# Bias rows stored head by head, four products in another order, sums ahead of splits, and a count of its own for one weight quarter, in a hybrid decoder layer on one Trainium2 core

## The reference

```python
h = rmsnorm(x, norm_g) * (1 + scale[:, None, :]) + shift[:, None, :]     # shift, scale, gate = split(c @ ada_w + ada_b)
q, kc, vc, ksl, vsl, kw, vw, gts, hc, bc, cc, z = split_proj(h @ w_in)
k_cmp, v_cmp = compress(kc, ...), compress(vc, ...)                      # silu(blocks @ w1) @ w2
o_attn = gates * (compressed attention, top-k selected attention, window attention)   # all with a T5 bias rel_bias
u = cc * hc
y_conv = bc * short_conv(u, conv_w)
x = x + gate * (concat([o_attn * silu(z_a), y_conv * silu(z_c)]) @ w_out)
y = rmsnorm(x, final_g)
```

## Time and profile before

| what | value |
|---|---|
| median of three runs | 1536.29 us (1535.63 to 1536.37) |
| the profiled execution | 1532.23 us |
| its span | 1530.4 us |
| TensorE matmul busy | 1433.0 us (94%) |
| VectorE, ScalarE, GpSimd busy | 964.0, 704.4, 234.7 us |
| chain that ended last | PE 80%, DVE 7%, DMA 5%, ACT 3% of the span |
| mean granted TensorE clock | 0.979 |

### The profile page before, as it was taken

One profiled execution on the slowest core, in us unless ns is written; L12 is line 12 of the kernel. 1 busy time (PEld: TensorE's weight loads), 2 busy tenths in 40 slices (PEclk: granted clock), 3 DMA queues, 4 the chain that ended last, 5 costly groups with the idle time before them and its releaser, 6 DMA issues.

```text
span 1530.4 us, 27904 instructions
## 1 busy us (share of the span) xinstructions
PE 1433.0 (94%) x10526; PEld 1236.4 (81%) x10526; DVE 964.0 (63%) x2312; ACT 704.4 (46%) x1546; POOL 234.7 (15%) x441
## 2 busy tenths in 40 slices
PE   5987998999999999969989999999999999999998
PEld 2876998999999999957767777777777766788886
DVE  2643768787787887848666666667567654653226
ACT  2421232423323223226567777777777765631111
POOL 1100010101101011031021242232222131000000
PEclk9998999999999999989999999999999999999999
DMA  9376123423333334297321141121121129963231
GB/s 345 99 137 126 28 84 90 117 60 96 86 75 105 78 90 112 62 316 237 111 91 43 29 108 56 43 70 47 33 57 30 30 74 357 265 207 98 82 98 35
DMA packets 169669, 164.76 MB, mean 108 GB/s; under 512 B 53644, under 2 KB 150028, under 8 KB 164160
## 3 DMA queue, kind: packets, MB, share of 16 engines
q1 hardware_dynamic: 153904, 94.11, 22.6%
q0 software_dynamic: 15632, 68.87, 14.9%
HBM read 131.27 MB, written 35.83 MB: 109 GB/s over the span
## 4 chain that ended last, share of the span: by engine, by line
PE 80%; DVE 7%; DMA 5%; ACT 3%; issue 3%; SPq 1%; DVEq 0%; POOL 0%; ACTq 0%
PE PS L1258 26%; PE PS L1619 11%; PE PS L1425 8%; PE PS L1390 7%; PE PS L1369 5%; PE PS L1307 4%; PE PS L1370 3%; PE PS L1472 2%; PE PS L1214 1%; DMA gw<-in_ada_w 1%; PE PS L1215 1%; PE PS L1216 1%; DMA adaw<-in_ada_w 1%; PE PS L1576 1%; DMA wr<-in_w_in 1%
## 5 line engine op out<-in xcount | busy, mean ns | idle before, releaser
L1258 PE MATMUL PS<-bo,wsl 128*128 128x264 f32 x4104 | 504.5, 286 | 11.1 <-DVE qp L2186 5.8
L1258 PEld LDWEIGHTS PS<-bo,wsl 128*128 128x128 f32 x4104 | 503.6, 190 | 12.2 <-DVE qp L2186 6.0
L1882 ACT ACTIVATE pr<-PS,nm 128x640 f32<-128x640 f32 (+7 forms) x256 | 181.0, 708 | 45.2 <-DVE nm L2392 42.6
L1715 ACT ACTIVATE wsl<-wsum 128x512 fp32r<-128x512 f32 x105 | 65.6, 630 | 231.9 <-DVE wsum L2107 231.9
L1905 ACT ACTIVATE ptt<-PS 128x512 f32<-128x512 f32 x264 | 149.6, 601 | 41.6 <-PE PS L1390 41.4
L1390 PE MATMUL PS<-ident,pr 128*128 128x128 f32 x1056 | 147.2, 274 | 0.0
L1425 PE MATMUL PS<-ptt,kvt 128*64 128x256 f32 x1056 | 136.7, 390 | 0.0
L1390 PEld LDWEIGHTS PS<-ident,pr 128*128 128x128 f32 x1056 | 122.4, 141 | 8.9 <-ACT ptt L1905 0.4
L1425 PEld LDWEIGHTS PS<-ptt,kvt 128*64 128x64 f32 x1056 | 66.9, 136 | 41.2 <-issue 16.5
L2392 DVE CUSTOM_DVE_ANT_0 PS<-PS,near,nm 128x256 f32<-128x256 f32 x192 | 94.7, 493 | 6.8
L2391 DVE TENSOR_REDUCE nm<-PS 128x1 f32<-128x128 f32 (+5 forms) x128 | 70.5, 551 | 39.2 <-PE PS L1370 38.7
(11 more groups left out here) (358 smaller groups left out, 2403.2 us busy)
## 6 DMA issues: line engine op xcount, KB each, us to landing
wr<-in_w_in SPq DMA_DIRECT2D x32, 512.0 KB, 5.6
adaw<-in_ada_w SPq DMA_DIRECT2D x8, 1024.0 KB, 9.5
wr<-in_w_in SPq DMA_DIRECT2D x32, 256.0 KB, 4.3
q_stacked<-qp POOLq DMA_DIRECT2D x64, 128.0 KB, 2.7
qb<-q_stacked SPq DMA_DIRECT2D x32, 256.0 KB, 3.1
mr<-mixed SPq DMA_DIRECT2D x16, 512.0 KB, 3.9
mixed<-yy POOLq DMA_DIRECT2D x16, 264.0 KB
xb<-in_x_prompt POOLq DMA_DIRECT2D x8, 512.0 KB, 4.7
```

Source lines behind the costliest of these rows:

```text
L1258: ins = pe.matmul(PS[:, 2 * q + c, 0:H // 2], w[:, x, kk, :], b[:, y, kk, c * H // 2:(c + 1) * H // 2], start=(first and kk == 0 and x == ...
L1882: act.activation(pr[r][:, h, 0:k], score_cols(b0, w), ACT.Exp, scale=-1.0, bias=nm[:, r, h:h + 1], accum_out=rsum[:, r, h:h + 1]).then_inc ...
```

## The change

The diff does five things. The line numbers of the changed file are some 9 to 14 higher than before's.

1. `rows` moves to partitions 64 to 79 of `kvs`, and the one store of 3072 KB becomes 16 stores of 192 KB, one for each head, issued by POOL in the pairs 4 to 19 (`store_bias(n - 4)` at step 4). ScalarE's wait for `row_st` is gone.
2. In pair 0 the first four products run in the order 2, 3, 0, 1. The wait for `kv_ev` moves to the second of them and that for `ada_ev` to the fourth.
3. The pieces of the sums: `ADDED` says at which step a piece is summed, `SPLIT` at which it is split. At a step the sum now comes ahead of the split of the piece before. Pieces 12 to 19 (now with O21 as 12 to 15 and O12 as 16 to 19) are summed before any of them is split, into `qp`, `ts`, `eg` and `er`; all have two instructions. The last split moves from step (3,2) to (2,6).
4. The first quarter of w1 of the keys counts on `wr_ld` (`load_w1(0, 0, wr_ld)`). TensorE waits for it ahead of step 0 and for the three others ahead of step 8.
5. The base of that semaphore in `wo_ld` falls from 64 to 48.

```diff
-        rows = sb("rows", [NH, XW], cx=cC)
...
+        rows = kvs[64:64 + NH, 0:XW]
...
-        wo_ld = list(zip(xp_ld + q_ld, [192, 192, 64, 64] + [128] * 4))
+        wo_ld = list(zip(xp_ld + q_ld, [192, 192, 48, 64] + [128] * 4))
...
-        PIECE = [(s_, k) for s_ in range(3) for k in range(HK)] + [(3, 2), (3, 3), (4, 2), (4, 3), (3, 0), (3, 1), (4, 0), (4, 1)]
-        PIECES = {(0, 0): 0, (0, 1): 1, (0, 2): 2, (0, 3): 3, (0, 4): 4, (0, 5): 5, (0, 6): 6, (0, 7): 7, (1, 0): 8, (1, 4): 9,
-                  (1, 5): 10, (1, 6): 11, (2, 2): 12, (2, 3): 13, (2, 4): 14, (2, 5): 15, (2, 6): 16, (2, 7): 17, (3, 0): 18, (3, 1): 19}
-        def op_scratch(x):
-            return (er, eg) if x % 2 else ts
+        PIECE = [(s_, k) for s_ in range(5) for k in range(HK)]
+        ADDED = {(0, 0): (0,), (0, 1): (1,), (0, 2): (2,), (0, 3): (3,), (0, 4): (4,), (0, 5): (5,), (0, 6): (6,), (0, 7): (7,),
+                 (1, 0): (8,), (1, 1): (9,), (1, 4): (10,), (1, 5): (11,), (1, 7): (16, 17), (2, 0): (18, 19), (2, 1): (12, 13), (2, 2): (14, 15)}
+        SPLIT = {(0, 1): (0,), (0, 2): (1,), (0, 3): (2,), (0, 4): (3,), (0, 5): (4,), (0, 6): (5,), (0, 7): (6,), (1, 0): (7,),
+                 (1, 1): (8,), (1, 4): (9,), (1, 5): (10,), (1, 6): (11,), (2, 3): (12, 13), (2, 4): (14, 15), (2, 5): (16, 17), (2, 6): (18, 19)}
+        def sum_ready(x):
+            return x + 1 if x < 12 else x + 5 if x < 16 else x - 3
+        def op_sum32(x):
+            if x < 12:
+                return (er if x % 2 else ts[0])[:, :]
+            return f32(qp[:, x - 12, :]) if x < 16 else (ts[1], eg, ts[0], er)[x - 16][:, :]
...
-            def load_w1(c, q):
+            def load_w1(c, q, landed=None):
                 src = (cmp_w1_k, cmp_w1_v)[c].rearrange("l (t p) c -> p (l t) c", p=P)
-                sp.dma_start(w1[c][:, 8 * q:8 * q + 8, :], src[:, 8 * q:8 * q + 8, :]).then_inc(xp_ld[2 + c], 16)
+                sp.dma_start(w1[c][:, 8 * q:8 * q + 8, :], src[:, 8 * q:8 * q + 8, :]).then_inc(landed or xp_ld[2 + c], 16)
...
-            load_w1(0, 0)
+            load_w1(0, 0, wr_ld)
...
-            po.wait_ge(tb_ev, 1)
-            rv = rows[:, :]
-            po.dma_start(rowd, bass.AP(rv.tensor, rv.offset, [list(rv.ap[0]), [0, P], [1, XW]])).then_inc(row_st, 16)
+            def store_bias(h):
+                rv = rows[h:h + 1, :]
+                po.dma_start(rowd[h:h + 1], bass.AP(rv.tensor, rv.offset, [list(rv.ap[0]), [0, P], [1, XW]])).then_inc(row_st, 16)
...
+                    if i == 4 and 4 <= n < 4 + NH:
+                        store_bias(n - 4)
...
-            pe.wait_ge(kv_ev, 2 * NTT)
...
-            pe.wait_ge(ada_ev, 8)
...
-                        k, op, out = PLAIN[i]
+                        k, op, out = PLAIN[(2, 3, 0, 1)[i] if n == 0 and i < 4 else i]
+                        if n == 0 and i == 1:
+                            pe.wait_ge(kv_ev, 2 * NTT)
+                        if n == 0 and i == 3:
+                            pe.wait_ge(ada_ev, 8)
...
-            pe.wait_ge(xp_ld[2], 64)
+            pe.wait_ge(wr_ld, raw_landed(NBLK - 1) + 16)
             for m in range(32):
+                if m == 8:
+                    pe.wait_ge(xp_ld[2], 48)
...
-                act.wait_ge(op_sum, x + 1)
-                if x >= 16:
-                    act.wait_ge(*made(2, 3))
-                elif x >= 12:
-                    act.wait_ge(*made(2, 3 if PIECE[x][0] == 4 else 1))
-                act.activation(bo[SUMS[PIECE[x][0]][0]][:, 0, PIECE[x][1], :], op_scratch(x)[0][:, :], ACT.Copy).then_inc(op_hi, 1)
+                s_, k = PIECE[x]
+                act.wait_ge(op_sum, sum_ready(x))
+                if x >= 12:
+                    act.wait_ge(*made(2, 3 if x >= 16 else 1))
+                act.activation(bo[SUMS[s_][0]][:, 0, k, :], op_sum32(x), ACT.Copy).then_inc(op_hi, 1)
...
-                    act.wait_ge(op_sum, 16 if half else 18)
+                    act.wait_ge(op_lo, 16)
...
-                    act.wait_ge(row_st, 16)
...
-                    if (n, i) in PIECES:
-                        op_high(PIECES[n, i])
+                    for x in ((ADDED if n < 2 else SPLIT).get((n, i if n < 2 else i + 1), ())):
+                        if (x < 12) == (n < 2):
+                            op_high(x)
...
-                t = op_scratch(x)
-                if x >= 2:
+                t, kept = op_sum32(x), f32(qp[:, k, :])
+                if 2 <= x < 12:
                     dve.wait_ge(op_lo, x - 1)
-                if x < 18:
-                    dve.wait_ge(op_kept, 1 if x < 12 else 2)
-                    first_, second = (f32(bo[a][:, 0, k, :]), f32(qp[:, k, :])) if s_ < 4 else (f32(qp[:, k, :]), f32(bo[b][:, 0, k, :]))
-                    link(dve.tensor_tensor(t[0][:, :], first_, second, op))
-                    dve.tensor_tensor(t[0][:, :], t[0][:, :], f32(bo[a if s_ < 4 else b][:, 1, k, :]), ALU.add).then_inc(op_sum, 1)
-                else:
-                    dve.tensor_tensor(t[0][:, :], f32(bo[a][:, 0, k, :]), f32(bo[b][:, 0, k, :]), op)
-                    link(dve.tensor_tensor(t[1][:, :], f32(bo[a][:, 1, k, :]), f32(bo[b][:, 1, k, :]), op))
-                    dve.tensor_tensor(t[0][:, :], t[0][:, :], t[1][:, :], ALU.add).then_inc(op_sum, 1)
+                if x >= 16:
+                    dve.wait_ge(op_lo, 12)
+                dve.wait_ge(op_kept, 1 if x < 12 else 2)
+                if 12 <= x < 16:
+                    dve.wait_ge(op_sum, 16)
+                own, first_, second = (b, kept, f32(bo[b][:, 0, k, :])) if s_ == 4 else (a, f32(bo[a][:, 0, k, :]), kept)
+                link(dve.tensor_tensor(t, first_, second, op))
+                dve.tensor_tensor(t, t, f32(bo[own][:, 1, k, :]), ALU.add).then_inc(op_sum, 1)
 
             def op_low(x):
-                (s_, k), t = PIECE[x], op_scratch(x)
+                s_, k = PIECE[x]
                 dst = bo[SUMS[s_][0]]
-                dve.wait_ge(op_sum, x + 1)
+                dve.wait_ge(op_sum, sum_ready(x))
                 dve.wait_ge(op_hi, 1 + x + 1)
-                dve.tensor_tensor(dst[:, 1, k, :], t[0][:, :], f32(dst[:, 0, k, :]), ALU.subtract).then_inc(op_lo, 1)
+                dve.tensor_tensor(dst[:, 1, k, :], op_sum32(x), f32(dst[:, 0, k, :]), ALU.subtract).then_inc(op_lo, 1)
...
-                    if (n, i) in PIECES:
-                        x = PIECES[n, i]
-                        if x:
-                            op_low(x - 1)
-                        if x == 12:
-                            whole(O11)
+                    for x in ADDED.get((n, i), ()):
                         op_add(x)
-                    if n == NPLAIN and i == 2:
-                        op_low(19)
+                    for x in SPLIT.get((n, i), ()):
+                        op_low(x)
+                    if n == 1 and i == 6:
+                        whole(O11)
```

More of the change, by code:

```diff
@@ L751, in _ @@
             sp.wait_ge(x3_t, 80)
-            sp.wait_ge(row_st, 16)
+            sp.wait_ge(row_st, 16 * NH)
             sp.dma_start(near[:, :, :], flat(rowd, P - 1, [(XW - 1, P), (P * XW, NH), (1, 2 * P)])).then_inc(c4_ld, 16)
@@ L1031, in _ @@
             po.memset(xp4[1][:, :, :, :], 0.0).then_inc(xz, 1)
-            po.wait_ge(row_st, 16)
             po.wait_ge(g_st, 16)
```

## The result

The changed kernel took 1575.18 us (median of four runs, 1574.57 to 1577.64), the kernel before 1535.96 us: a ratio of 1.0259, 95% interval 1.0241 to 1.0277. I had said 1513, and at most 1528. It is slower by 39 us where I forecast 23 less. The profiled execution has a span of 1573.1 us against 1530.4.

A forecast was written before the change was run, and what follows sets the result against it. TensorE, busy 94% of the span, was taken as the bound, so only its waits could be won: 13.7 + 4.1 + 11.9 + 13.5 = 43.2 us won, 20 lost, 23 less, 1513 us on the median; range 1490 to 1528.

The forecast's parts named there:

- Part 1a: Gates steps at the start: without the 3072 KB store the slice of ada_w lands on time, winning 13.7 us.
- Part 2: First four products of the projection: the new order removes TensorE's wait for the gate sums, winning 4.1 us.
- Part 3: Pieces of the sums in the projection: TensorE's waits up to product (3,3) and lower clock go, winning 11.9 us.
- Part 4: Start of the compression: TensorE no longer stalls for w1 of the keys ahead of step 0, winning 13.5 us.
- my 677.5: Forecast time of compression step 8: 664.5 + 12.7 for steps 0 to 7 at full clock + 0.3.
- Part 1b: The 16 bias stores in the projection: 8 us each, holding up weight loads queued behind them, 20 us lost.
- The single ones: Stores in pairs 5, 8, 11, 14 and 17, ahead of weight loads: 16 us of waits and some 4 of lower clock.
- The ten in twos: Stores issued behind four q_stacked stores, the load nearly in: put at 0, at most 2 us a group.
- the 43.2 won: Forecast sum of the four gains over the whole kernel: 13.7 + 4.1 + 11.9 + 13.5 us.
- Rival C: Each bias store holds the weights for 16 us or more: 80 us, giving 1573 us, slower; chance 0.05.
- Rival A: The bias stores in the projection are nearly free, 2 us of loss, giving 1495 us; chance 0.33.

The follow-up runs named there:

- the kernel with 16 partitions: Changed kernel, each 192 KB bias store taking all 16 heads 8 times instead of one head 128 times: 1499.87 us, ratio 0.9778 to the kernel before.

## Why the prediction was wrong, point by point

**Part 1a, the store out of the start: right.** 13.7 forecast, 13.9 measured; that they agree to 0.2 us is luck, the scatter is some 5. The gates steps of the changed kernel are 10.6 us apart.

**Part 2, four products: right.** 4.1 forecast. The wait of 4.11 us is gone; the clock behind it, which I left out, adds one or two us (6.2 measured).

**Part 3, the pieces: right.** 11.9 forecast, 11.3 measured by the medians and 14.3 by the traces. VectorE is in time at (3,3).

**Part 4, w1: too high by 10 us.** 13.5 forecast, 3.4 measured. The step that failed is "what is late next". I named the second gathered quarter and put it just in time. What was late was the wait of VectorE and ScalarE for the tail's store, which costs TensorE 3.3 to 3.8 us and, with the clock behind it, nearly 5 (28.5 against 23.8). Another 5 us are missing even with that mended (23.8 us from the last product to step 8, where my 677.5 less 659.0 is 18.5). Two causes show in the rows. The rows of the keys came later behind the last product (TensorE waits for them 3.48 us in that kernel, 1.54 before), and the first steps ran below full clock: from the four transposes ahead of step 0, at 635.31, to step 1 at 640.60 it is 5.3 us, 0.56 of them a wait, where I had 2.1. I had assumed full clock behind short waits.

**Part 1b, the 16 stores: the step that turned the sign.** I put their loss at 20 us; it is 75.6. The time of a store was right (8 forecast, 8.7 alone and 9.2 in company). The single ones were nearly right: I had 16 us of waiting and 4 of clock, measured are 21.0 (19.0 at the five pairs that I had priced, 2.0 at pairs 4 and 5, for which I had nothing) and some 7. The waits at pairs 6 and 12 are 5.93 and 3.06; I had 6.5 for the pair behind store 5, and 1.9. The ten in twos are the failure. The sentence was: "The ten stores issued in twos come behind four stores of `q_stacked`, when the load is nearly in; I put them at 0, at most 2 us a group." They cost 48.4 us, 9.7 a group. The load was not nearly in: SP issues it at 278.13 us, in the midst of POOL's four `q_stacked` stores (277.15 to 279.49), and the two bias stores follow 1.4 us later. Its first half came through in 5.8 us. The second half, under way for 0.9 us, took 18.0 us instead of the 7.7 us that it takes beside the queries alone: it was held up for 10 more. I had looked for what is issued *behind* a store in the order of issue, and taken what is issued *ahead* of it as safe. It isn't.

The trace of before had the rows to see this. Its DMA view of 298.0 to 301.5 us shows the load in company with the queries (last row: the load's second half alone, from the view of 300.4 to 301.2 us):

```profile
wr<-in_w_in SPq DMA_DIRECT2D x2, 512.0 KB, 7.0
q_stacked<-qp POOLq DMA_DIRECT2D x4, 128.0 KB, 4.7
...
wr<-in_w_in SPq DMA_DIRECT2D x1, 512.0 KB, 7.7
```

and VectorE already waited for that load:

```profile
307.97 1.29 DVE L2107 TENSOR_TENSOR wsum<-wr 128x512 f32<-128x512 f32 x2 [0.92 <-DMA wr<-in_w_in]
```

An idle time of 0.92 us in front of this sum says that the load has no slack in these pairs. With the issue times and VectorE's lead from the changed kernel's trace, my own price of a store would then have done: two stores at 8 us from 279.5 end at 295.5 (the load landed at 296.6), where 278.5 + 7.7 = 286.2 was due; of these 9.3 us of delay VectorE's lead takes off some 2 (it waited 9.67 us at pair 7, TensorE 7.49). Five times 7 us is 35 (35.4 measured), with the 20 of the singles 55, more than the 43.2 won: slower, near 1536.3 - 43.2 + 55 = 1548 us, an estimate in hindsight, before any lower clock behind the twos.

**The rivals.** Rival C, the slower one, gave 1573 us, within 2 us of the result, at a chance of 0.05. Its mechanism (the loads held up by the stores) is the one that acted, but not with its price: it needed 16 us a store, and said that it decides from about 11 us. At 9 us a store it was decided all the same, since two in a row count as one of 17. That its time comes so near is luck: of its 80 us it put 55 on the singles and 25 on the twos; measured are 28.1 and 48.4, and the four gains come to 35 us, not 43. The range left it out, because I had priced the twos in the forecast at nothing and only in C at something; the position and the price were tied together where they were two unknowns. Rival A (stores nearly free, 1495) is what the kernel with 16 partitions shows, not this one: 1499.9.

## What to carry to other kernels

Before a store is put beside the loads of a loop, ask what is in flight when it runs, not only what is issued after it; the half of a load that was issued 0.9 us ahead took 18.0 us instead of 7.7. Let a store that repeats a row take its rows from partitions that lie at least 4 apart, or from 16 of them, and not from one: here it made the difference between 1575 and 1500 us at equal bytes. When a long stall is taken away, list every wait of the engines that feed the bottleneck, counts for outputs included; here a store of 64 KB was next.

## What the runs showed of the hardware

- One SBUF partition as the source of a 192 KB store gives 8.7 us to landing with nothing beside it. In company, one partition and four adjacent ones both gave POOL's queue 27 to 29 GB/s, four that were 4 apart some 165 GB/s.
- With four adjacent partitions the 16 engines were busy for POOL's queue only 47% of the time, with one partition 92%, and yet the load of the weights crept in both: 0.02 MB in 7 us and 0.05 MB in 10 us. So it isn't the engines' busy share alone that holds the load up. Why the load does not fill the half that reads as free isn't shown by these rows and stays open. The Trainium skill, "DMA: Bandwidth & Descriptors", section "Queues, rings and completion order", has an engine take turns between queues by packets. The counts of packets in the rows above agree with that in all three cases: 91 of the stores and 98 of the load with one partition, 41 and 35 with four adjacent ones, 114 and 118 with four that are 4 apart. The load's packets are the small ones (0.05 MB in 98) and the stores' the large ones (0.29 MB in 91), so a load that gets one packet for each slow packet of a store creeps. That this is the whole cause is argued from the counts, not shown by a run of its own.
- The 5 us behind a wait of 7.49 us had a granted clock of 0.57, those behind 3.66 us 0.50, those behind 3.06 us 1.00.
